# The first normalisation of a two-layer hybrid block: features instead of tokens, and the root's factor after the first product

## The reference, cut to what matters

```python
def rms_norm(x, w):
    y = x * lax.rsqrt(jnp.mean(x * x, axis=-1, keepdims=True) + NORM_EPS)
    return y * w

for l in range(2):                                # x: 256 tokens x 1024 features
    h = rms_norm(x, norm_mix[l])
    proj = h @ w_in[l]                            # 1024 x 7688
    (dq, dk, dv, dz, da, db, mq, mk, mv, lx, ly, gates) = split_columns(proj)
    y_dn = gated_deltanet(dq, dk, dv, dz, da, db, ...) @ dn_out[l]   # uses silu(dz)
    y_mb = moba_attention(mq, mk, mv) @ mb_out[l]
    y_lru = rg_lru_branch(lx, ly, ...) @ lru_out[l]
    x = x + (gated sum of the three) @ w_o[l]
    h = rms_norm(x, norm_ffn[l])
    x = x + (silu(h @ gate) * (h @ up)) @ ffn_down[l]
return rms_norm(x, norm_final)
```

## Time and profile before

| what | value |
|---|---|
| median of 3 runs | 900.74 us (900.73 to 900.75) |
| the profiled execution | 900.52 us |
| its span, first to last instruction | 898.7 us |
| mean granted TensorE clock | 0.998 |
| busy: PE, weight loads, DVE, ACT, POOL | 889.2, 759.1, 670.5, 513.2, 2.4 us |
| DMA | 182.65 MB, 203 GB/s on the mean |

### The profile page before, as it was taken

The page is one execution under the profiler, slowest core; times in us unless marked ns, Lnnn a source line. Parts: engine busy times, 40 slices in busy tenths (PEclk is TensorE's granted clock), DMA queues, the critical chain, the costliest instruction groups (busy, mean ns, idle before and its releaser), DMA issues.

```text
span 898.7 us, 13817 instructions
## 1 busy us (share of the span) xinstructions
PE 889.2 (99%) x5392; PEld 759.1 (84%) x5392; DVE 670.5 (75%) x1111; ACT 513.2 (57%) x877; POOL 2.4 (0%) x6
## 2 busy tenths in 40 slices
PE   9999999999999999999999999999999999999997
PEld 6999898888888888888889998988888888888885
DVE  6879877788968665756778898767988675666656
ACT  7586656785446444444566766567744544444434
POOL 0000000000000000000000000000000000000000
PEclk9999999999999999999999999999999999999999
DMA  8646547867665677777755374488667467767671
GB/s 307 210 153 181 196 128 200 244 227 236 210 208 175 205 206 236 220 235 239 229 177 168 117 221 154 126 242 256 220 212 232 162 204 234 242 202 246 217 205 47
DMA packets 137376, 182.65 MB, mean 203 GB/s; under 512 B 90464, under 2 KB 96224, under 8 KB 137312
## 3 DMA queue, kind: packets, MB, share of 16 engines
q1 hardware_dynamic: 137168, 181.52, 64.1%
q10 hardware_dynamic: 144, 0.26, 0.1%
HBM read 170.21 MB, written 11.53 MB: 202 GB/s over the span
## 4 chain that ended last, share of the span: by engine, by line
PE 94%; DVE 4%; ACT 2%; issue 0%; ACTq 0%; DVEq 0%
PE bank L508 7%; PE bank L506 7%; PE bank L507 7%; PE bank L634 7%; PE bank L636 7%; PE bank L635 7%; PE bank L724 6%; PE bank L409 6%; PE bank L410 5%; PE bank L411 5%; PE bank L450 5%; PE bank L448 5%; PE bank L449 5%; PE bank L437 2%; PE bank L438 2%; PE bank L436 2%
## 5 line engine op out<-in xcount | busy, mean ns | idle before, releaser
L960 ACT CAST whi<-raw 128x1024 fp32r<-128x1024 f32 x290 | 303.4, 1053 | 287.3 <-PE bank L508 95.2
L1309 DVE TENSOR_TENSOR wlo<-raw,whi 128x1024 fp32r<-128x1024 f32 x290 | 347.1, 1216 | 65.2 <-ACT whi L960 62.9
L409 PE MATMUL bank<-ahi,whi 128*128 128x256 f32 x448 | 129.7, 289 | 0.8 <-DVE tmp L1359 0.8
L410 PE MATMUL bank<-alo,whi 128*128 128x256 f32 x448 | 126.7, 283 | 0.0
L411 PE MATMUL bank<-ahi,wlo 128*128 128x256 f32 x448 | 126.6, 283 | 0.0
L506 PE MATMUL bank<-whi,ahi 128*128 128x512 f32 x288 | 112.2, 390 | 0.0
L508 PE MATMUL bank<-whi,alo 128*128 128x512 f32 x288 | 112.1, 389 | 0.0
L507 PE MATMUL bank<-wlo,ahi 128*128 128x512 f32 x288 | 112.0, 389 | 0.0
L634 PE MATMUL bank<-whi,ahi 128*128 128x512 f32 x272 | 108.1, 398 | 0.1
L636 PE MATMUL bank<-whi,alo 128*128 128x512 f32 x272 | 106.1, 390 | 0.0
L635 PE MATMUL bank<-wlo,ahi 128*128 128x512 f32 x272 | 106.0, 390 | 0.0
(11 more groups left out here) (306 smaller groups left out, 1326.8 us busy)
## 6 DMA issues: line engine op xcount, KB each, us to landing
raw<-stream_dram SPq DMA_DIRECT2D x292, 512.0 KB, 4.7
turned_dram<-proj SPq DMA_DIRECT2D x144, 32.0 KB, 1.7
proj<-turned_dram SPq DMA_DIRECT2D x18, 256.0 KB, 4.5
proj<-gbias_dram SPq DMA_DIRECT2D x12, 256.0 KB, 4.4
probs_dram<-proj SPq DMA_DIRECT2D x8, 192.0 KB, 4.3
proj<-probs_dram SPq DMA_DIRECT2D x2, 768.0 KB, 5.0
par<-params_dram SPq DMA_DIRECT2D x2, 556.5 KB, 6.3
vturn_dram<-proj SPq DMA_DIRECT2D x8, 128.0 KB, 3.0
```

Of the source, the lines that this page charges most:

```text
L409: pe.matmul(dst, whi_of(m)[:, wcol], hi, start=first, stop=False, skip_group_check=True)
L410: pe.matmul(dst, whi_of(m)[:, wcol], lo, start=False, stop=False, skip_group_check=True)
L960: act.copy(whi_of(m), raw_of(m)).then_inc(*AC.up(("hi", m), "w"))
L1309: dv.tensor_tensor(wlo_of(m), raw_of(m), whi_of(m), ALU.subtract).then_inc(*DV.up(("lo", m), "w"))
```

## The change

x arrives transposed by the host (`xT`, 128 features by 8 x 256 tokens), in the same place, as 344 KB (with norms and identity) and then 768 KB. Nothing is normalised first. ScalarE rounds xT times the norm's weight (`unscaled`, into free slots of `bhi`), VectorE (for six of the eight feature tiles) and GpSimd (for two) make the low parts, and z is multiplied from these unscaled values. The squares are taken from xT by ScalarE in four 128 x 512 instructions, added up by GpSimd in three, and summed over partitions by four matmuls with ones (into bank 3). ScalarE takes a Sqrt, VectorE a reciprocal and one refinement; the factor enters z when it leaves its bank (`tz`: a scaled copy and a scaled Tanh for each half of the tokens instead of one Tanh). For the other projections the factor is spread over the features' partitions by four transposes of a broadcast column, into banks 2 and 6; VectorE multiplies half of xT with it, GpSimd the other half after a copy of bank 6 by ScalarE; ScalarE rounds the result (`x_round_first`, at k = 1 and 2) and VectorE makes the low parts (`x_split_first`). At k = 4 and 5 TensorE waits for these one feature tile at a time. The small product for a and b goes from k = 3 to 5, and all that follows from it by one half as well. GpSimd makes the low part of weight half 4. x itself, by tokens, is loaded (1024 KB) at SP's k = 6. Two of the six warming products are removed, and the short one goes ahead of the wait.

```diff
+        xT = head[:, NHEAD:NHEAD + 2 * D].rearrange("p (k t) -> p k t", k=KT)
...
+        def low_by(m):
+
+            return (PO if m == RING - 1 else DV).at("w", ("lo", m))
+
+        def alone(kt):
+            return 4 + kt
...
-            sp.dma_start(head[:, 0:NHEAD + D], head_in[:, 0:NHEAD + D]).then_inc(loaded_x[0], 16)
+            sp.dma_start(head[:, 0:NHEAD + 2 * T], head_in[:, 0:NHEAD + 2 * T]).then_inc(loaded_xT[0], 16)
             load(0)
-            sp.dma_start(head[:, NHEAD + D:], head_in[:, NHEAD + D:]).then_inc(loaded_x[1], 16)
+            sp.dma_start(head[:, NHEAD + 2 * T:], head_in[:, NHEAD + 2 * T:]).then_inc(loaded_xT[1], 16)
             load(1)
-            sp.wait_ge(loaded_x[0], 16)
+            sp.wait_ge(loaded_xT[0], 16)
...
+                    if l == 0 and k == 6:
+                        sp.wait_ge(*DV.at(l, ("xs", 1)))
+                        sp.wait_ge(*PO.at(l, ("xs", 3)))
+                        sp.dma_start(x, x_in).then_inc(loaded_x, 16)
...
+                    if l == 0 and k in (4, 5):
+                        m = l * NH + k
+                        pe.wait_ge(*AC.at(l, ("mix", "hi", kt)))
+                        for n in range(2):
+                            pe.matmul(dst[:, n * T:(n + 1) * T], whi_of(m)[:, cols(2 * i + n)], ahi[:, kt, :], start=kt == 0 and n == 0, stop=False, skip_group_check=True)
+                            pe.matmul(dst[:, n * T:(n + 1) * T], wlo_of(m)[:, cols(2 * i + n)], ahi[:, kt, :], start=False, stop=False, skip_group_check=True)
+                        pe.wait_ge(*DV.at(l, ("mix", "lo", kt)))
+                        for n in range(2):
+                            ins = pe.matmul(dst[:, n * T:(n + 1) * T], whi_of(m)[:, cols(2 * i + n)], alo[:, kt, :], start=False, stop=kt == KT - 1, skip_group_check=True)
+                        continue
...
+            def z_unscaled(l):
+
+                def group(q, stationary, moving):
+                    for t in range(2):
+                        for kt, col in ((2 * q, slice(0, 512)), (2 * q + 1, slice(512, 1024))):
+                            if t == 0 and stationary is blo:
+                                pe.wait_ge(*(PO if kt > 5 else DV).at(l, ("alone", "lo", kt)))
+                            elif t == 0:
+                                pe.wait_ge(*AC.at(l, ("alone", "hi", kt)))
+                            ins = pe.matmul(bank[4 + t][:, :], stationary[:, alone(kt), t * P:(t + 1) * P], moving[:, col],
+                                            start=kt == 0 and stationary is bhi and moving is highs[0], stop=kt == KT - 1 and stationary is blo,
+                                            skip_group_check=True)
+                        if q == 3 and stationary is blo:
+                            ins.then_inc(*PE.up(("z", t)))
+                    return ins
+
+                highs = [whi_of(q) for q in range(4)]
+                for q in range(4):
+                    pe.wait_ge(*AC.at("w", ("hi", q)))
+                    group(q, bhi, highs[q])
+                    if q == 0:
+                        group(q, blo, highs[q])
                     wait_split(l, q)
+                    ins = group(q, bhi, wlo_of(q))
+                    if q == 2:
+                        pe.wait_ge(*PO.at(l, "squares"))
+                        for t in range(2):
+                            for b in range(2):
+                                last = exact(bank[3][:, 8 * t:8 * t + 8], proj[:, SQX + b, t * P:(t + 1) * P], sm["sso"], b == 0, b == 1)
+                        last.then_inc(*PE.up("sum"))
                     if q == 3:
+                        pe.wait_ge(*DV.at(l, ("mix", "nr")))
+                        for b in (2, 6):
+                            for t in range(2):
+                                last = pe.transpose(bank[b][:, t * P:(t + 1) * P], sm["nr"][:, t:t + 1].broadcast_to([P, P]), ident[:, :])
+                            last.then_inc(*PE.up(("roots", b)))
+                    if q:
+                        ins = group(q, blo, highs[q])
+                    if q < 3:
                         ins.then_inc(*PE.up(("bulk", q)))
...
-                if k == 3:
...
+                if k == (3 if l else 5):
...
-                if k == 4:
+                if k == (4 if l else 6):
...
-            for i in range(6):
+            for i in range(4):
                 exact(bank[7][:, :], tmp[:, 0, 0:P], tmp[:, 0, :])
-            pe.wait_ge(loaded_x[0], 16)
+            exact(bank[7][:, 0:T], tmp[:, 0, 0:P], tmp[:, 0, 0:T])
+            pe.wait_ge(loaded_xT[0], 16)
             for l in range(L):
                 PE.layer = l
-                if l == 0:
-                    x_transpose(l, "mix", 0)
-                    exact(bank[7][:, 0:T], tmp[:, 0, 0:P], tmp[:, 0, 0:T])
...
+                def unscaled(*kts):
+                    for kt in kts:
+                        act.activation(bhi[:, alone(kt), :], xT[:, kt, :], ACT.Copy, scale=nrm[:, kt:kt + 1]).then_inc(*AC.up(("alone", "hi", kt)))
+
+                def squared(*pairs):
+                    for p in pairs:
+                        act.activation(tiles(SQX + 2 * p, 2), xT[:, 2 * p:2 * p + 2, :], ACT.Square).then_inc(*AC.up(("squared", p)))
+
+                act.wait_ge(*DV.at(l, "ones"))
+                act.activation(sm["rt"], sm["sso"][:, 0:1], ACT.Sqrt).then_inc(*AC.up())
+                act.wait_ge(*DV.at(l, "norms"))
+                unscaled(0, 1)
+                squared(0)
                 hi(0)
+                act.wait_ge(loaded_xT[1], 16)
+                unscaled(2, 3)
+                squared(1)
                 hi(1)
+                squared(2, 3)
                 hi(2)
+                unscaled(4, 5, 6, 7)
                 hi(3)
+                hi(4)
+                act.wait_ge(*DV.at(l, "mean"))
+                act.activation(sm["hr"], sm["wn"], ACT.Sqrt).then_inc(*AC.up("root"))
+
+            def x_round_first(l, kts):
+                if kts[0] == 0:
+                    act.wait_ge(*PE.at(l, ("roots", 6)))
+                    act.copy(tiles(RSB, 1)[:, 0, :], bank[6][:, 0:T]).then_inc(*AC.up("roots"))
+                for kt in kts:
+                    act.wait_ge(*(DV if kt < 4 else PO).at(l, ("xs", kt // 2)))
+                    act.activation(ahi[:, kt, :], tiles(XS + kt, 1)[:, 0, :], ACT.Copy, scale=nrm[:, kt:kt + 1]).then_inc(*AC.up(("mix", "hi", kt)))
...
-                if k == 5:
+                if k == (5 if l else 6):
...
-                        act.activation(flat(tiles(ZT + 2 * t, 2)), bank[4 + t][:, :], ACT.Tanh, scale=0.5).then_inc(*AC.up(("tz", t)))
+                        if l == 0:
+                            act.wait_ge(*DV.at(l, "hz"))
+                            act.activation(flat(tiles(TZ + 2 * t, 2)), bank[4 + t][:, :], ACT.Copy, scale=sm["nr"][:, t:t + 1]).then_inc(*AC.up())
+                        act.activation(flat(tiles(ZT + 2 * t, 2)), bank[4 + t][:, :], ACT.Tanh,
+                                       scale=0.5 if l else sm["s2r"][:, t:t + 1]).then_inc(*AC.up(("tz", t)))
...
-                    hi(l * NH + k + AHEAD)
+                    if l == 0 and k in (1, 2):
+                        x_round_first(l, range(4 * k - 4, 4 * k))
+                    if l or k:
+                        hi(l * NH + k + AHEAD)
...
+                if l == 0:
+                    dv.wait_ge(loaded_x, 16)
...
+                def low(*kts):
+                    for kt in kts:
+                        dv.wait_ge(*AC.at(l, ("alone", "hi", kt)))
+                        step(dv.scalar_tensor_tensor(out=blo[:, alone(kt), :], in0=xT[:, kt, :], scalar=nrm[:, kt:kt + 1],
+                                                     in1=bhi[:, alone(kt), :].bitcast(F32), op0=ALU.mult, op1=ALU.subtract), ("alone", "lo", kt))
+
+                low(0, 1)
                 lo(0)
+                low(2, 3)
                 lo(1)
                 lo(2)
+                low(4, 5)
+                dv.wait_ge(*PE.at(l, "sum"))
+                step(dv.tensor_scalar(sm["wn"], bank[3][:, 0:16].rearrange("p (t m) -> p t m", m=8)[:, :, 0], MEAN, EPS * D * MEAN, ALU.mult, ALU.add), "mean")
                 lo(3)
+                y, w, u = sm["nr"], sm["wn"], sm["un"]
+                dv.wait_ge(*AC.at(l, "root"))
+                step(dv.reciprocal(y, sm["hr"]))
+                settle()
+                step(dv.tensor_tensor(u, y, w, ALU.mult))
+                settle()
+                step(dv.tensor_tensor(u, u, y, ALU.mult))
+                settle()
+                step(dv.scalar_tensor_tensor(out=y, in0=u, scalar=-3.0, in1=y, op0=ALU.add, op1=ALU.mult), ("mix", "nr"))
+                settle()
+                step(dv.tensor_scalar(sm["s2r"], y, 0.5, None, ALU.mult), "hz")
+                dv.wait_ge(*PE.at(l, ("roots", 2)))
+                for p in range(2):
+                    step(dv.tensor_tensor(tiles(XS + 2 * p, 2), xT[:, 2 * p:2 * p + 2, :], over(bank[2][:, 0:T], 2), ALU.mult), ("xs", p))
+
```

(76 more changed lines are left out.)

40 lines of the change are left out of this document (5 added, 35 removed).

## The result

The changed kernel takes 903.33 us (median of 11 executions, 902.72 to 905.03); the kernel before took 900.73 beside it (ten of its eleven executions lie between 900.54 and 900.81; one took 3084.91, and the median isn't touched by it). The ratio is 1.003, with an interval of 1.0023 to 1.0038: 2.6 us slower. The profiled execution took 902.97 with a span of 901.2, against 900.52 and 898.7 before.

The account below looks back on a forecast made before the run. TensorE was taken as busy 889.2 of 898.7 us, leaving only the start, with VectorE's list next. TensorE alone would gain 1.9 us, of which VectorE's list passes 0.44: 900.3 against the median of 900.74, range 898.9 to 902.0.

Parts of the forecast that it names:

- the paragraph on GpSimd: Start, during z: GpSimd's sums, low parts and products, all hidden by z if it runs beside VectorE undisturbed.
- The sum: Whole kernel: profiled 900.52 less 0.44, so 900.1, or 900.3 against the median of 900.74.
- The rival on the other side: Start: GpSimd holds VectorE up, `lo(3)` waiting for `lo(4)`; 901.2, with the second product 901.7. Chance 0.28.
- The turning point of 0.44: Start: the delay of VectorE by GpSimd at which the forecast gain turns, 0.44 us.
- the signs of being wrong: GpSimd above 1.2 us for 512 columns, or holding low parts; first z matmul after 8.5; broadcast near 47.2 or after 49.
- GpSimd's own prices: Start: GpSimd's two-input instructions taken as 1.1 us for 512 columns and 2.2 for 1024.
- The main case, VectorE's list binds: Start to gcol's broadcast: VectorE's list lets only 0.44 us of gain through; 900.3, range 899.8 to 900.9. Chance 0.40.
- TensorE's lead of 1.9: Up to k = 8: TensorE alone would have gained 1.9 us, k = 7 ending at 35.3 instead of 37.2.
- TensorE's path binds alone: Start: if z's exit or low parts come earlier, up to 1.9 us survive; 899.0, range 898.6 to 899.8. Chance 0.16.
- First data late: Start: the 768 KB land after 8.4, or half 1 after 9.7, delaying z and ScalarE; 901.5. Chance 0.10.
- The table load: ScalarE, before Exp after the Sqrt: 1.28 us; with a gap 2.66, turning the 0.44 gain into a 0.9 loss.
- The clock: During z: TensorE might run part at 1.2 GHz, three groups costing 2.7 us; 903. Chance 0.06.

Follow-up runs that it names:

- GpSimd out: Changed kernel with all eight of GpSimd's new additions, subtractions and products on VectorE, without bank 6 and its copy: 900.36 us, ratio 0.9999 to the kernel before.
- the late work: Changed kernel with half 4's low part and the second rounding's two products moved from GpSimd to VectorE: 901.30 us, ratio 1.0006 to the kernel before.
- the early work: Changed kernel with the three additions of squares and low parts 6 and 7 moved from GpSimd to VectorE: 903.86 us, again 902.54.
- the best kernel: GpSimd out, plus lo(3) ahead of the mean, an early Exp for the table, and the first convolution ahead of abT: 899.80 us, ratio 0.9992 to the kernel before.
- the kernel with only `lo(4)` moved: Changed kernel with weight half 4's low part made by VectorE behind the factor instead of by GpSimd: 902.26 us, ratio 1.0018 to the kernel before.
- twelve in a row: Kernel before plus twelve one-input GpSimd instructions of 256 columns on scratch: 900.97 us; with twelve two-input ones instead: 902.75 us (one run each).
- one variant: Changed kernel with sums of squares and low parts 6 and 7 on VectorE, half 4's low part and late products still on GpSimd: 903.86 us, again 902.54.

## Why the prediction was wrong

**The step that failed** is the paragraph on GpSimd, "all hidden by z, if it runs beside VectorE undisturbed". It doesn't, and all that follows from it fell:

| | forecast | changed | GpSimd out |
|---|---|---|---|
| z starts | 8.1 | 7.69 | 7.67 |
| low part of half 1 there | 12.0 | 13.1 | 12.1 |
| factor | 18.9 | 21.9 | 18.8 |
| k = 4 starts | 21.0 | 23.78 | 21.45 |
| product for a and b starts | 27.15 | 31.30 | 28.43 |
| abT starts | 31.9 | 36.11 | 33.25 |
| k = 8 starts | 36.35 | 39.90 | 37.03 |
| broadcast | 48.55 | 51.83 | 48.97 |

In the right column, without GpSimd, the landmarks lie within 0.1 of the forecast from half 1's low part to the factor, and 0.4 behind it at the broadcast. In between they don't fit as well: k = 4 starts 0.45 late, the product for a and b and abT 1.3 late, k = 8 0.7 late. The broadcast fits better than TensorE's path does, since it hangs on VectorE's columns (48.68, forecast 48.5). That kernel is also not the one forecast: VectorE has some five us more to do in it.

Of the 3.28 us between forecast and changed kernel at the broadcast, 2.86 go away with GpSimd: 1.85 with the late work (51.83 to 49.98), 1.01 with the early work (49.98 to 48.97). Taken in the other order, and without the clock's fall, the early work is worth 0.9. The sum had this term at nothing.

**The rival on the other side** had the mechanism and the page right, with 0.28, and was under-sized. It priced one meeting, `lo(3)` inside `lo(4)` (0.9), and the second product (0.5), for 901.2 to 901.7. It left out that the exclusion works on every instruction with two inputs in SBUF, small ones and GpSimd's own too. `lo(3)` itself was nearly free (1.30); what paid was the product of two numbers behind it, 2.15, and `lo(1)` and the low parts early in z, 1.0, for which the forecast had no meeting at all, and 1.0 among the second rounding's four. The turning point of 0.44 was passed by 2.8 us. Of the signs of being wrong that the prediction named, two that belong to it came: GpSimd's 512 columns took more than 1.2 us, and the broadcast started after 49. The range ended at 902.0, since I held 0.9 for the most that one such meeting could cost and took them one at a time.

**GpSimd's own prices** were 1.29 for 512 columns where I took 1.1, and 2.39 for 1024 (the undisturbed one at 16.36) where I took 2.2. Right enough; the row of the mask was a fair guide. Not the sizes failed but what else they stopped.

**The main case, VectorE's list binds**, was right in form, with waits too large. With GpSimd out TensorE stands 0.3 before k = 8 for the convolution, where 1.05 was forecast, and 0.15 before the broadcast, where 0.4 was, and the chain from abT through the decay to gcol runs as laid out. TensorE's lead of 1.9 had already shrunk: it waits 0.59 for the first tile of the second rounding and 0.59 for `lo(5)`, both behind VectorE, and k = 5 runs from 25.46 to 28.43 (forecast 24.3 to 27.15). Even in the best kernel abT ends at 33.93, 1.5 behind the forecast's 32.4, so 1.5 of the 1.9 that TensorE alone would have gained aren't there, and no kernel here reached the 899.0 of the rival "TensorE's path binds alone".

**First data late**: no. The second transfer landed at 1.62 + 6.8 = 8.4, as forecast, and the first at 0.72 + 3.1 = 3.8. Half 1's cast let TensorE wait 0.17 here, up to 1.0 in another execution of a variant. **The table load** took 1.28 with no gap before it:

```profile
27.29 1.98 ACT L996 CAST whi<-raw 128x1024 fp32r<-128x1024 f32 x2
29.29 1.28 ACT L1107 ACT_TABLE_LOAD   x1
```

**The clock** was given 0.06, for 903, by a slow z. The measured 903.33 lies next to that number by chance: z ran at the full rate throughout. A fall later on, behind the waits at 20 to 26, is likely in two executions of eleven; it would explain the tail up to 905.0, not the median.

**Open** is in part why the kernel with only `lo(4)` moved lies 1.0 above the one that has the late products moved too (902.26 and 901.30; the profiled ones 902.28 and 901.17), though their broadcasts differ by 0.14. In the medians, four executions at a lower mean clock count; the other seven lie 0.5 above. In the profiles the difference grows at two places: from 0.17 to 0.51 near 174.7, where TensorE waits 0.24 behind the late bias, and from 0.53 to 0.95 between 419 and 432, where the profile names a wait of 0.18.

## What to carry to other kernels

Here GpSimd's two-input work was free only where VectorE meanwhile read one operand from PSUM. Its one-input work cost between nothing (VectorE's two low parts at 9.00 took their usual 0.89 beside it) and 0.2 an instruction, and twelve in a row about a third of what twelve with two inputs did. A GpSimd instruction with two SBUF inputs and a VectorE instruction with two are best counted as one after the other, and a tiny VectorE instruction that meets a long one of GpSimd can pay nearly the whole of it; VectorE, which did the same additions in half the time, was the better place even with a full list. And when a start is rearranged, add up the new waits of TensorE in it: behind 1.2, 0.3 and 1.4 us within five, some executions had a spell at half clock on top. A landmark, too, stands only for what comes before it: 1.2 us were lost 125 us behind the one used here.

## What the hardware showed that was not expected

- A VectorE product of 128x2 (0.16 us) stood 2.0 us behind a GpSimd subtraction of 128x1024.
- GpSimd takes longer with one input and a scalar than with two inputs: 1.04 to 1.15 us against 0.89 to 0.96 for 256 columns. Yet VectorE's instructions lose 0.1 to 0.2 to the one and 0.4 to 0.5 to the other.
- The granted clock fell to 0.50 for some 3 us in both profiles of one variant, behind waits that the changed kernel's profile has too, which stays at 1.00. By the mean clock of the executions it was 7 of 16 of that variant, 2 of 11 of the changed kernel, and 4 of 11 of a kernel that doesn't wait at the factor.
